# A ring of expert weights: a narrow expert's visit moved from the sixth place to the fifth

## The reference

```python
logits = t @ w_router                              # 256 x 8
top_val, top_idx = lax.top_k(logits, 2)
top_w = softmax(top_val)
gates = sum over k of top_w[:, k] * one_hot(top_idx[:, k], 8)
for e in range(8):                                 # w1, w3: 1024 x 3584, w2: 3584 x 1024
    hid = silu(t @ e_w1[e]) * (t @ e_w3[e])
    y  += (hid @ e_w2[e]) * gates[:, e][:, None]
out = rmsnorm(h + y, final_norm)
```

## Time and profile before

| what | value |
|---|---|
| median of 3 runs | 1863.05 us (1862.99 to 1865.78) |
| the profiled execution | 1862.72 us |
| its span, from first to last instruction | 1860.9 us |
| TensorE's mean granted clock | 0.989 |
| PE busy, share of the span | 93% |
| DVE, ACT, POOL busy | 35%, 29%, 4% |
| read from HBM | 496.84 MB |

### The profile page before, as it was taken

How to read it: one execution, slowest core, us unless ns; L and a number is a source line. 1 busy time by engine, 2 the same in 40 slices (tenths; PEclk the granted TensorE clock), 3 DMA queues, 4 the chain that set the end, 5 groups by cost and what they waited for, 6 DMA issues and landing times.

```text
span 1860.9 us, 37427 instructions
## 1 busy us (share of the span) xinstructions
PE 1739.1 (93%) x16339; PEld 1117.6 (60%) x16339; DVE 649.8 (35%) x1122; ACT 530.9 (29%) x920; POOL 65.2 (4%) x64
## 2 busy tenths in 40 slices
PE   6999998999989989999988999999999999988886
PEld 3776677886668779998876454435435344423323
DVE  3664855235775765556664001010000100000001
ACT  3435834334564654334443000001000010000001
POOL 0120000011200000000001000000000000000000
PEclk9999999999999999999999999999999999999999
DMA  8362014753424635555529999999999999999996
GB/s 329 135 227 90 2 62 157 222 167 85 80 79 156 188 122 183 194 189 190 183 110 365 326 415 423 413 424 411 425 414 423 387 408 424 410 425 414 424 422 273
DMA packets 166923, 501.33 MB, mean 269 GB/s; under 512 B 27000, under 2 KB 54048, under 8 KB 150384
## 3 DMA queue, kind: packets, MB, share of 16 engines
q1 hardware_dynamic: 163824, 491.82, 70.4%
q0 software_dynamic: 1888, 6.62, 1.1%
q10 hardware_dynamic: 1056, 0.57, 0.1%
HBM read 496.84 MB, written 2.12 MB: 268 GB/s over the span
## 4 chain that ended last, share of the span: by engine, by line
PE 71%; issue 12%; DVE 6%; ACT 5%; DMA 4%; SPq 1%; POOL 1%; ACTq 0%; POOLq 0%; DVEq 0%
PE bank L2581 21%; PE bank L2021 10%; PE bank L2023 10%; PE bank L2022 10%; PE bank L2574 8%; DMA ring_t<-in_e_w 2%; ACT w_hi L844 1%; SPq L757 1%; DMA ring_h<-in_e_w 1%; DVE w_lo L1244 1%; PE bank L2200 1%; PE bank L2189 1%; PE bank L2214 1%; PE bank L2043 1%; PE bank L2527 1%
## 5 line engine op out<-in xcount | busy, mean ns | idle before, releaser
L1244 DVE TENSOR_TENSOR w_lo<-raw,w_hi 128x2048 fp32r<-128x2048 f32 x98 | 224.7, 2295 | 196.0 <-ACT w_hi L844 195.9
L2021 PE MATMUL bank<-h_hi,w_hi 128*128 128x256 f32 (+1 forms) x864 | 261.8, 303 | 4.9 <-DVE w_lo L1244 3.1
L2023 PE MATMUL bank<-h_hi,w_lo 128*128 128x256 f32 (+1 forms) x864 | 258.8, 300 | 0.0
L2022 PE MATMUL bank<-h_lo,w_hi 128*128 128x256 f32 (+1 forms) x864 | 258.6, 299 | 0.0
L844 ACT ACTIVATE w_hi<-raw 128x2048 fp32r<-128x2048 f32 x98 | 186.8, 1909 | 160.2 <-PE bank L2023 111.5
L2581 PE MATMUL bank<-ring_w,xe 128*32 128x512 f32 (+1 forms) x1920 | 188.3, 543 | 9.7 <-DMA ring_w<-in_e_w 9.6
L2021 PEld LDWEIGHTS bank<-h_hi,w_hi 128*128 128x128 f32 x864 | 165.8, 192 | 14.0 <-DVE w_lo L1244 5.7
L2022 PEld LDWEIGHTS bank<-h_lo,w_hi 128*128 128x128 f32 x864 | 165.8, 192 | 5.6 <-issue 0.2
L2023 PEld LDWEIGHTS bank<-h_hi,w_lo 128*128 128x128 f32 x864 | 165.7, 192 | 5.0
L1873 DVE TENSOR_TENSOR act_f<-act_s,bank 128x512 f32<-128x512 f32 (+1 forms) x40 | 22.7, 616 | 402.8 <-PE bank L2581 402.8
L2581 PEld LDWEIGHTS bank<-ring_w,xe 128*32 128x32 f32 x1920 | 61.6, 111 | 134.4 <-issue 106.2
(11 more groups left out here) (344 smaller groups left out, 2174.3 us busy)
## 6 DMA issues: line engine op xcount, KB each, us to landing
ring_w<-in_e_w SPq DMA_DIRECT2D x72, 1024.0 KB, 18.1
ring_h<-in_e_w SPq DMA_DIRECT2D x64, 1024.0 KB, 17.9
ring_t<-in_e_w SPq DMA_DIRECT2D x48, 1024.0 KB, 15.3
raw<-in_e_w SPq DMA_DIRECT2D x40, 1024.0 KB, 22.5
ring_w<-in_e_w SPq DMA_DIRECT2D x48, 768.0 KB, 13.8
raw<-in_w SPq DMA_DIRECT2D x33, 1024.0 KB, 5.1
raw<-in_w_qkv SPq DMA_DIRECT2D x24, 1024.0 KB, 5.1
ring_h<-in_e_w SPq DMA_DIRECT2D x32, 768.0 KB, 17.6
```

What stands on the lines that cost most here:

```text
L1244: nc.vector.tensor_tensor(w_lo[:, split_slot(m), :], raw_unit(m), w_hi[:, split_slot(m), :].bitcast(F32), ALU.subtract).then_inc(lo_ready, 1)
L2021: nc.tensor.matmul(out_, a_hi, b_hi, start=start, stop=False)
L2022: nc.tensor.matmul(out_, a_hi, b_lo, start=False, stop=False)
L2023: return nc.tensor.matmul(out_, a_lo, b_hi, start=False, stop=stop)
```

## The change

The fifth and the sixth visit change places. Before, the widths of visits 0 to 7 are W N W W W N N N, now they are W N W W N W N N. `RANK_AT` moves along, so each expert keeps its width: the expert of rank 5 is visited in visit 4, that of rank 3 in visit 5.

With that, the loop body for visit 6 follows a wide visit, while for any further turn of the loop it would follow a narrow one. One body must serve both, so the loop's `combine` always adds three groups. For this the loop's visits also build, turn and copy three groups of picks (`picked`), and the third must be empty for a narrow visit: `route` gets 96 more columns, in which the slots 64 to 95 hold the number -1e4, which no token has. In the last visit `combine` adds three groups too; its third group multiplies the zeros that visit 6 left in `pick_gt`. `route` is therefore 416 floats wide instead of 320, all tiles placed behind it move by 384 bytes in every partition, and `ring_t` by 400. As the program's allocation places them, `raw`, `ring_w` and `ring_h` began at a multiple of 512 bytes before and begin 384 past one now; `ring_t` began 104 bytes past one before, and 504 past one now.

```diff
-RANK_AT = [0, 4, 1, 2, 3, 5, 6, 7]
-FIRST_VISITS = [WIDE, NARROW, WIDE, WIDE, WIDE, NARROW]
+RANK_AT = [0, 4, 1, 2, 5, 3, 6, 7]
+FIRST_VISITS = [WIDE, NARROW, WIDE, WIDE, NARROW, WIDE]
...
-    row = np.concatenate([np.arange(P), tie, thresholds, np.tile(e, OVERS), RANK_AT])[None, :]
+    row = np.concatenate([np.arange(P), tie, thresholds, np.tile(e, OVERS), RANK_AT,
+                          np.where(np.arange(SLOTS) < MORE, np.arange(SLOTS), -1e4)])[None, :]
...
-        sb("gap_before_ring_t", [P, 1526 + 92])
+        sb("gap_before_ring_t", [P, 1622])
...
-            def visit(v, groups, last):
+            def visit(v, groups, last, picked):
...
-                for t in range(groups):
+                for t in range(picked):
                     ins = nc.scalar.activation(pick_gt[:, t, :], bank[t][:, 0:TOK], ACT.Copy)
...
-                visit(v, NARROW, False)
+                visit(v, NARROW, False, WIDE)
...
-                    dst = pick_g[:, t, 0:groups * P].rearrange("p (a b s) -> p a b s", a=groups, b=4)
-                    src = slot_number[:, 0:groups * TILE].rearrange("p (a s) -> p a s", a=groups).unsqueeze(2)
+                    dst = pick_g[:, t, 0:picked * P].rearrange("p (a b s) -> p a b s", a=picked, b=4)
+                    own = slot_number if groups == WIDE else route[:, R_NARROW:R_END]
+                    src = own[:, 0:picked * TILE].rearrange("p (a s) -> p a s", a=picked).unsqueeze(2)
...
-                        combine((FIRST_VISITS + [NARROW])[v - 1] if isinstance(v, int) else NARROW)
+                        combine(FIRST_VISITS[v - 1] if isinstance(v, int) else WIDE)
```

More of the change, by code:

```diff
@@ L95 @@
 R_RANK = R_EXPERT + OVERS * EXP
-R_END = R_RANK + EXP
+R_NARROW = R_RANK + EXP
+R_END = R_NARROW + SLOTS
 K_ID, K_NEAR, K_STRICT, K_NEGS, K_END = 0, 128, 192, 320, 448
@@ L1209, in _ @@
             for v, groups in enumerate(FIRST_VISITS):
-                visit(v, groups, False)
+                visit(v, groups, False, groups)
             act.wait_ge(sem("routed"), 1)
@@ L1213, in _ @@
             with act.Fori(len(FIRST_VISITS), last_visit) as v:
-                visit(v, NARROW, False)
+                visit(v, NARROW, False, WIDE)
             with act.Fori(last_visit, last_visit + 1) as v:
-                visit(v, NARROW, True)
+                visit(v, NARROW, True, NARROW)
             squares("n6", TT, lambda t: (sem("x_added"), 4 * t + 4), lambda t: xs[:, TT + t, :])
@@ L1836, in _ @@
             link(nc.vector.tensor_reduce(ids_f[:, EXP:VISITS], over_tmp[:], AX.X, ALU.add))
-            link(nc.vector.tensor_tensor(base_hot[:], by_rank(rank[:]), route[:, R_RANK:R_END].unsqueeze(2).broadcast_to([P, EXP, EXP]),
+            link(nc.vector.tensor_tensor(base_hot[:], by_rank(rank[:]), route[:, R_RANK:R_NARROW].unsqueeze(2).broadcast_to([P, EXP, EXP]),
                                          ALU.is_equal))
@@ L1884, in visit @@
                 for t in range(TT):
-                    dst = pick_g[:, t, 0:groups * P].rearrange("p (a b s) -> p a b s", a=groups, b=4)
-                    src = slot_number[:, 0:groups * TILE].rearrange("p (a s) -> p a s", a=groups).unsqueeze(2)
-                    ins = nc.vector.tensor_scalar(dst, src.broadcast_to([P, groups, 4, TILE]), now[:, t:t + 1], now[:, 4 + t:5 + t],
+                    dst = pick_g[:, t, 0:picked * P].rearrange("p (a b s) -> p a b s", a=picked, b=4)
+                    own = slot_number if groups == WIDE else route[:, R_NARROW:R_END]
+                    src = own[:, 0:picked * TILE].rearrange("p (a s) -> p a s", a=picked).unsqueeze(2)
+                    ins = nc.vector.tensor_scalar(dst, src.broadcast_to([P, picked, 4, TILE]), now[:, t:t + 1], now[:, 4 + t:5 + t],
                                                   ALU.is_equal, ALU.mult)
```

## The result

The changed kernel is slower: a median of 1872.25 us (1870.77 to 1872.65, 6 runs) against 1863.42 us for the kernel before (1861.57 to 1865.78, 6 runs), a ratio of 1.0049 with a 95% interval of 1.0039 to 1.0059. That is 8.8 us more, where 4.4 us less was forecast. The profiled execution took 1872.28 us, its span is 1870.4 us (before 1862.72 and 1860.9), the mean granted clock 0.989 as before.

A forecast was written before the change was run, and what follows sets the result against it. Loads at near one rate and TensorE in wide visits were taken to bound the kernel. 1862.72 - 4.4 + 0 + 0 + 0 = 1858.3 us, plus 0.33 us to the median: 1858.6 us, range 1856.8 to 1862.4 us.

The forecast's parts named there:

- The bounds and the course of the visits: Experts' visits: TensorE catches up in narrow visit 4, waits some 7 us; wide visit 5 starts without lag, ends 9.4 us behind.
- the clock: Rival: waits at visit 4's end lower the granted clock ahead of wide visit 5, giving 1867 us; chance 0.02.
- The added work: Third group of picks and combine in visits 6 and 7, where engines have idle time: cost 0, uncovered 2.1 us.
- the wider constant: Load of route with 30% more bytes, issued well before the routing reads it: cost 0, uncovered 1.5 us.
- The placement: Ring slots moved by 384 or 400 bytes: cost 0, from ring_t and ring_h units 2.46 and 2.45 us apart.
- its rival: Moved ring slots make loads slower, 0.03 us per unit, giving 1866.8 us; chance 0.06.
- The upper bound: Placement cost of at most 0.03 us per 1 MB unit, 8.2 us over 273 units in moved slots.
- The estimate by that page: Unaligned ring slots move 128 extra bytes in 8192, 1.6% of all loads; kernel would end at about 1869 us.
- The -4.4 us: Exchange of visits 4 and 5 recovers the loads' deficit in visit 4: 4.4 us faster, bounds 3.9 and 4.6 us.
- The third of my three ways: Visit 4's loss from TensorE's starts: visit 6 at 1636.83 against 1632.9 for four visits of 106.58 us, so 3.9 us.
- The line of loads at 106.6 us a visit: Reference for TensorE's lag: loads at full rate from 1206.6 us, with visit 3 9.4 and visit 4 19.6 us behind.

The follow-up runs named there:

- e15: Kernel before with the new visit order alone, every tile in its old place and no added work: 1862.18 us, ratio 0.9992.
- e3: Changed kernel with 32 more unused floats behind route, so all ring slots stand 512 bytes behind those of before: 1862.09 us, ratio 0.9991.
- e1: Kernel before with unused floats putting every tile behind route where the changed kernel has it: 1870.65 us, ratio 1.0039.
- e2: Kernel before with everything behind route moved by 512 bytes: 1862.78 us, ratio 0.9996.
- e6: Kernel before with everything behind route moved by 256 bytes: 1862.33 us, ratio 0.9998.
- e7: Kernel before with everything behind route moved by 128 bytes: 1872.03 us, ratio 1.0051.
- e5: Kernel before with raw and ring_w (9 slots) moved by 384 bytes, the other slots keeping their distance to a boundary: 1873.34 us, ratio 1.0058.
- e12: Kernel before with ring_w alone (6 slots) moved by 384 bytes: 1871.12 us, ratio 1.0037.
- e14: Kernel before with ring_h (4 slots) and the small tiles behind it moved by 384 bytes: 1868.69 us, ratio 1.0025.
- e9: Kernel before with 8 more loads per visit in visits 1 to 7, each one partition x 6 KB on one engine: 1864.89 us, ratio 1.0001.
- e10: Kernel before with 16 more loads per visit in visits 1 to 7, each one partition x 6 KB on one engine: 1873.72 us, ratio 1.0055.
- e11: Kernel before with 8 more loads per visit in visits 1 to 7, each 16 partitions x 6 KB: 1916.23 us, ratio 1.0276.

## Why the prediction was wrong

**The bounds and the course of the visits were right.** TensorE's wide visits kept their 116.0 us (after a narrow one) and 116.7 us (after a wide one); visit 4 became narrow and ended in waits for loads; visit 5 started without lag and visit 6 where TensorE's times put it, 116.0 us later; the queue did not run dry in visit 4; the clock stayed at 1.00 in the periods from visits 2 to 4, which end at 1576.6 us. The added work and the wider constant cost nothing that can be told: e15, which has neither, is as fast as e3, which has both (0.9992 and 0.9991).

**The placement was the step that failed first.** I costed it at 0 from two rows of `ring_t` and `ring_h`, and gave its rival 0.06. `ring_t` does stand off its boundary at a small price, so the row was right, and the conclusion for the other thirteen slots was not: they cost 8.9 us in e1. The upper bound that I worked out beside it, 0.03 us per unit and 8.2 us in all, comes close. Even so the rival's 1866.8 us is 5.4 us short of the measured 1872.25, because it kept the gain of 4.4 us.

The Trainium skill's page "DMA: Bandwidth & Descriptors", section "How a descriptor splits into AXI transactions", has a descriptor that starts off a 256-byte boundary also move the bytes below its start. The estimate by that page was 1.6% of all loads, about 10.7 us in the prediction's sum, with every piece taken as 8192 bytes. The trace has 14071 packets of 8192 bytes between 1100 and 1800 us, but also 13858 of 6144 and 21504 of 4096; with 128 bytes more for each, the estimate by the page is 2.2%, some 15 us, and 8.9 were measured. The dependence on the 256-byte boundary is as the page has it, by e1, e2, e6 and e7 for the thirteen slots together, where I had let one pair of rows overrule it. The size isn't: `ring_t` and raw alone cost far less than the rule asks, and that the extra bytes are the cause is not shown by any run.

**The -4.4 us was the second.** Its size came from the rate of 16 engines summed up. The deficit was there (403 for 419 GB/s) and the exchange did remove it, but what it was worth to the kernel was some 0.5 to 1 us: 0.5 in TensorE's starts, 0.7 in the last shares and 0.9 in the experts' part of e15, 1.0 and 1.2 us in the medians of e15 and e3. The rest was idle time of engines that were ahead. The third of my three ways, the one from TensorE's starts, could have told. Four visits took 1636.83 - 1206.58 = 430.25 us, 107.6 us each. I subtracted 106.6, the period of a later visit. In e15, where no queue ran dry, three visits from 1206.6 (its copy of visit 2 comes 0.04 us after before's) to 1528.67 take 107.4 us each. Four of them are 429.4, and before lost 0.8 us against that. The line of loads at 106.6 us a visit was wrong for the same reason: the last shares come 107.5 us apart up to visit 6, and only from visit 6 to visit 7 105.9.

Split in this way, which adds up by its making, the profiled difference is +8.9 (placement, e1) - 0.5 (837.3 to 836.8, the exchange on top of it) + 1.1 (first copy at 1033.56 instead of 1032.50, ahead of the experts) = +9.5 us, which is 1870.4 - 1860.9.

**What stays open.** Which engines are the late ones and why; the records of the landings don't say which engine a share was on. Why `ring_t`'s 104 bytes are cheap, and why raw alone costs less than it does beside ring_w. Why a small load on sixteen engines costs 0.95 us. And why the stage ahead of the experts was slower in e5, e12 and e14.

No kernel here beats the one before by more than a measurement can tell. e3 and e15 are the fastest, 0.08 to 0.09% less with intervals that touch 1.

## What to carry to other kernels

When an edit makes a constant wider, everything allocated behind it moves; keep large DMA destinations at the old distance to a 256-byte boundary with a few unused floats, before judging the edit itself (the same change was 0.49% slower without them; with them it was 0.09% faster, which can't be told from no change). When transfers are spread over 16 engines, price a dip in GB/s by when the consumer could start its next unit, not by the missing bytes: the dip may be only the idle time of the engines that were ahead. And where small effects are compared, split the profile at the start of the stage that the edit is about.

## What the runs showed of the hardware

- Loads whose destination starts 128 bytes past a multiple of 256 in each partition (moves by 128 and by 384 bytes) made the experts' part slower by 8.9 to 9.4 us, with 273 of its 336 MB of units placed so: 0.03 us on a 2.45 us unit. Moves by 256 and 512 bytes cost nothing. One group of tiles at 104 bytes past a boundary cost 0.5 us against aligned, a third or less of the price of the others.
- The 16 shares of one unit land far apart. The spread is 3 to 7 us in before, and up to 11 us in e15, which has no dip in GB/s. In the dip of before the mean share lost 4.6 us and the last one 0.7.
- Small loads on one engine were free as long as they took less than what that engine gained on the last in a visit: 1.8 us of them for 2 us in e9. With 3.7 us in e10 a visit took 109.2 us instead of 107.5, as 105.5 + 3.7 has it.
- A load of 16 partitions x 6 KB cost 0.95 us in e11, four times what its bytes would take on 16 engines.
